# Local attention's probabilities turned on VectorE and by DMA in place of TensorE, on one Trainium2 core

## Chip, cores, metric

One core of one Trainium2 chip runs the whole program in one launch. The metric is device time in microseconds (us); a kernel's time is the median of its runs.

## What is computed

The reference is a two-layer encoder trunk (512 tokens of 1024 channels). Each layer normalises x, projects it with one input matrix, runs three branches on the pieces and adds the output projection back:

```python
h = rms_norm(x, g); z = h @ w_in
ya = neighbourhood_attention(aq, ak, av, rpb) * silu(ag)
yb = dilated_attention(rotary(bq), rotary(bk), bv) * silu(bg)
yc = conformer_conv(ca, cb, ...) * silu(cg)
x = x + concat([ya, yb, yc]) @ w_out
...
p = softmax(s.reshape(B, H, GRID_W, kh * kw), axis=-1)
return einsum('bhcij,ibhcjd->bhcd', p, v_win)
```

The neighbourhood ("local") attention has 4 heads: each token of the 8 x 64 grid looks at 8 rows and 16 columns around it, with a learned bias. The dilated attention has 6 heads over all 512 keys with a table of counts. A final RMSNorm ends the program. All of it is float32.

## The kernel before

**Tiles.** Every large product is made in three passes with the operands split in a high and a low part (`products`, L560 to L562: hi*hi, hi*lo, lo*hi), each pass a 128x128 weight block against 512 columns. A layer has 40 tiles: 29 of the input projection, 3 pointwise tiles of the convolution (29 to 31), 8 of the output projection (32 to 39). One tile is 24 matmuls of 512 columns (9 for a pointwise tile). In the last layer the output projection is turned round (`row_products`, L622 to L624: activations stationary, weights moving), in parts by pairs of weight blocks.

**Steps.** The queue of each engine is written out by hand. Nine tiles come first; from then on work goes by steps n = 0 to 42: TensorE does half a tile in each of the steps 0 to 39 (tile 9 + n // 2) and a pointwise tile in each of 40 to 42. Attention runs beside it, one unit a step: a unit is one head and 128 queries, 8 units are a pair of heads, 24 units of the dilated pairs 0 to 2 come first, then 16 of the local pairs 3 and 4 (units 24 to 39). For a local unit there are 256 keys.

**A unit's way.** TensorE makes the scores of four units at a time (`scores`, L670, after steps 3, 7, ... 35). VectorE adds bias or table and takes the maximum into a place of the ring `prob` (`maxima`, L1226, two units in every even step); ScalarE takes exp (`exps`, L846) and, one step later, scales by VectorE's reciprocal (`norm`, L853); two steps after its start TensorE turns the 128-column blocks of the probabilities into the bank `tp` (`turn`, L684), ScalarE copies them into `pT` (`empty_turn`, L871), and once a pair is there TensorE multiplies it with v (`values`, L703 for dilated pairs, L709 for local ones), after the steps 10, 18, 26 and 34 and, for the last pair, after step 42. VectorE multiplies the result by the gate (`gated`, L1247, L1251). The gated pair is split for the output projection by `y_hi` (ScalarE, L884) and `y_lo` (VectorE, L1266) in the order `K_ORDER`.

**Queues.** GpSimd's queue (POOL) loads the weights that aren't split on the chip: `load_hi` (L997) into `w_hi`, as soon as the tile five before is done; ScalarE negates a copy of it into `w_lo` (`negate`, L783); `load_lo` (L1002) then adds the weights onto it by DMA. The order in POOL's queue is fixed, each entry waits in its turn. SyncE's queue (SP) loads the raw weights of the first nine tiles into `pT`'s space, swaps rows for the rotary step (L464), stores v's turned blocks to DRAM and loads them back in another order (`store_v` L468, `load_v` L482), loads the biases of the local units into a ring of two (`load_bias`, L496) and in the last layer moves blocks of x (`move_x`, L489). `gf` (1024 columns) holds the final norm's gains, loaded ahead of the last layer's steps.

**VectorE's own turning** exists already for v (`vector.transpose`, L1148) and x (L1186): it turns blocks of 32x32 only; the blocks then have to change places by DMA.

The waits between engines are semaphores; VectorE's tile work is in `empty_tile` (L1103 to L1155), the convolution's taps in `conv_taps` (L1206).

Of the kernel before, what the change touches and what calls it, by code (L numbers as in the profile page):

```python
# [26 lines left out]
P = 128  # L27
SEQ = 512
# [50 lines left out]
DUNITS = DPAIRS * UPP  # L79
Y_OF_PAIR = [2, 3, 4, 0, 1]  # L80
K_ORDER = [2, 3, 4, 0, 5, 6, 1, 7]
# [7 lines left out]
NEG_TILE = 896  # L89
PREP = 8 + CT * TAPS + 4 * CT  # L90
# [13 lines left out]
X_ORDER = [list(range(KD))] + [K_ORDER] * (DEPTH - 1)  # L104
# [6 lines left out]
Y_BEFORE_W = 6  # L111
# [22 lines left out]
def build(nc, xT, w_in, w_pw, w_out, prm, gfin, nabias, lncnt, rope, out):  # L134
    with ExitStack() as ctx:
# [77 lines left out]
        bias_in = [sem(f"bias_in{i}") for i in range(2)]  # L213
# [34 lines left out]
        p_ready = sem("p_ready")  # L248
        t_ready = sem("t_ready")
# [132 lines left out]
        ROW_PARTS = [(0, [0]), (0, [1]), (0, [2]), (0, [3]), (1, [0]), (1, [1]), (1, [2, 3])]  # L382
        LAST = DEPTH - 1
# [10 lines left out]
        X_TILES = [(0, KD // 2), (KD // 2, KD)]  # L394
        X_BLOCKS = {26: 0}
# [42 lines left out]
        def _(sp):  # L438
# [44 lines left out]

            def move_x(half, i):
# [7 lines left out]
            def load_bias(l, un):  # L492
                b = un - DUNITS
# [16 lines left out]
            for l in range(DEPTH):  # L510
# [4 lines left out]
                if l == LAST:  # L515
                    sp.dma_start(gf[:, :], gfin).then_inc(gf_in, 16)
                for n in range(UNITS):
# [33 lines left out]
        def _(pe):  # L551
# [52 lines left out]
            def row_products(half, kps):  # L604
# [3 lines left out]
                elif kps[0] == 0:  # L608
                    pe.wait_ge(pt_ready, UNITS * DEPTH)
# [65 lines left out]
            def turn(l, n):  # L675
# [3 lines left out]
                if UNITS * l + n:  # L679

                    pe.wait_ge(pt_ready, UNITS * l + n)
                blocks = QT if g < DPAIRS else NKEY // P
                for k in range(blocks):
# [8 lines left out]
            def values(l, g):  # L692

                pe.wait_ge(pt_ready, UNITS * l + UPP * (g + 1))
# [10 lines left out]
                else:  # L705
                    for b in range(QT):
                        for half in range(2):
# [17 lines left out]
            for l in range(DEPTH):  # L725
# [15 lines left out]
                for n in range(SLOTS):  # L741
# [11 lines left out]
                    if n >= UPP + LAG and n % UPP == LAG and n < UNITS + LAG:  # L753
                        values(l, n // UPP - 1)
                    if LAG <= n < UNITS + LAG:
# [7 lines left out]
                values(l, PAIRS - 1)  # L763

                if l == LAST:
                    for half, kps in ROW_PARTS:
                        row_products(half, kps)
                    break
                c = N_IN + CT
                open_tile(l, c)  # L770
                products(c, act_hi, act_lo, order=K_ORDER, ready=(ylo_ready, KD * l))
                for c in range(N_IN + CT + 1, N_CH):
                    open_tile(l, c)
                    products(c, act_hi, act_lo, order=K_ORDER, used=act_used if c == N_CH - 1 else None)
# [3 lines left out]
        def _(act):  # L778
# [63 lines left out]
            def exps(l, n):  # L842
                w = SEQ if n < DUNITS else NKEY
# [694 lines left out]
```

## Time and profile before

| | before |
|---|---|
| time, median of 3 runs | 530.83 us (530.13 to 532.09) |
| the profiled execution's own time | 532.22 us |
| its span | 530.2 us |
| TensorE busy | 519.1 us (98%) |
| VectorE, ScalarE, GpSimd busy | 369.8, 279.3, 135.5 us |
| DMA moved | 92.32 MB, mean 174 GB/s |

The span is the stretch that the profiler saw; the 2.0 us between it and the execution's time lie outside. "Busy" is the time in which an engine works on at least one instruction. Engines overlap, so the shares don't add up; a share near the whole span says that shortening anything else is worth something only if this engine waits for it. A row of the profile's groups gives line, engine, operation, `out<-in` by the program's names, the count, busy time and mean duration, and behind the second bar how long the engine was idle just before such instructions and who ended that.

### The profile page before, as it was taken

The numbers are of one execution on the slowest core, as the hardware profiler recorded it, in microseconds if no ns is written. First come the engines' busy times: TensorE is split into PE (matmuls) and PEld (weight loads), VectorE is DVE, ScalarE is ACT, GpSimd is POOL, SyncE is SP. The second block draws the span as 40 slices with busy tenths as digits, with TensorE's granted clock in tenths as the row PEclk, the third lists the DMA queues.
The fourth block names the chain that finished last, engine by engine and source line by source line (L and its number), as shares of the span: only waits on it lengthen the run. The fifth ranks groups of instructions, "written<-read, shape, count | busy, mean of one in ns | idle before, by whom it ended". The sixth has DMA issues, their size and how long they took to land.

```text
span 530.2 us, 7797 instructions
## 1 busy us (share of the span) xinstructions
PE 519.1 (98%) x2846; PEld 406.2 (77%) x2846; DVE 369.8 (70%) x721; ACT 279.3 (53%) x535; POOL 135.5 (26%) x168
## 2 busy tenths in 40 slices
PE   8999999999999999999999999999999999999995
PEld 6888777587786887888888877877768678777884
DVE  6979697989984627611539969979999646546134
ACT  6713376565765558623423315756657656654314
POOL 0114232122133312324411233122122352123201
PEclk9999999999999999999999999999999999999999
DMA  8625688766675875799502479975785969669963
GB/s 285 270 79 138 158 196 203 164 168 160 151 194 137 216 176 117 182 279 269 155 6 99 108 168 217 205 174 133 169 185 137 229 163 253 133 133 231 229 139 159
DMA packets 39014, 92.32 MB, mean 174 GB/s; under 512 B 5440, under 2 KB 16960, under 8 KB 38976
## 3 DMA queue, kind: packets, MB, share of 16 engines
q0 software_dynamic: 17856, 61.09, 51.6%
q1 hardware_dynamic: 20832, 30.54, 17.8%
q8 instruction: 23, 0.38, 0.3%
q10 hardware_dynamic: 288, 0.19, 0.1%
q14 instruction: 15, 0.12, 0.1%
HBM read 81.84 MB, written 4.72 MB: 163 GB/s over the span
## 4 chain that ended last, share of the span: by engine, by line
PE 79%; DMA 9%; DVE 6%; issue 2%; SPq 1%; ACT 1%; POOL 1%; POOLq 0%; DVEq 0%; ACTq 0%
PE acc L560 17%; PE acc L562 17%; PE acc L561 17%; PE tp L684 5%; PE misc L703 4%; PE sc L670 4%; DMA sq<-sq 3%; DMA w_hi<-w_in 2%; DMA bias<-nabias 1%; PE sc L622 1%; PE sc L623 1%; PE sc L624 1%; DMA v_way<-vB 1%; PE sc L560 1%; PE sc L562 1%
## 5 line engine op out<-in xcount | busy, mean ns | idle before, releaser
L560 PE MATMUL acc<-act_hi,w_hi 128*128 128x512 f32 x480 | 195.2, 407 | 0.0
L562 PE MATMUL acc<-act_lo,w_hi 128*128 128x512 f32 x480 | 187.7, 391 | 0.0
L561 PE MATMUL acc<-act_hi,w_lo 128*128 128x512 f32 x480 | 187.3, 390 | 0.0
L562 PEld LDWEIGHTS acc<-act_lo,w_hi 128*128 128x128 f32 x480 | 90.1, 188 | 20.0
L560 PEld LDWEIGHTS acc<-act_hi,w_hi 128*128 128x128 f32 x480 | 90.2, 188 | 17.8 <-issue 1.4
L561 PEld LDWEIGHTS acc<-act_hi,w_lo 128*128 128x128 f32 x480 | 90.5, 188 | 17.0 <-issue 0.5
L783 ACT ACTIVATE w_lo<-w_hi 128x1024 fp32r<-128x1024 f32 (+1 forms) x62 | 61.9, 999 | 42.1 <-DMA w_hi<-w_out 37.3
L846 ACT ACTIVATE prob<-prob,nmx 128x512 f32<-128x512 f32 (+1 forms) x80 | 50.5, 631 | 38.6 <-DVE nmx L1226 38.6
L1206 DVE SCALAR_TENSOR_TENSOR y<-ub,par,y 128x512 f32<-128x512 f32 x90 | 67.3, 748 | 0.0
L1206 DVE SCALAR_TENSOR_TENSOR ub<-ub,par 128x512 f32<-128x512 f32 x84 | 65.8, 783 | 0.0
L1002 POOL DMA_DIRECT2D w_lo<-w_in x40 | 35.8, 895 | 113.1 <-ACT w_lo L783 112.4
L871 ACT ACTIVATE pT<-tp 128x512 f32<-128x512 f32 (+1 forms) x80 | 40.2, 502 | 44.5 <-PE tp L684 44.4
L853 ACT ACTIVATE prob<-prob,rden 128x512 f32<-128x512 f32 (+1 forms) x80 | 50.4, 630 | 22.9 <-DVE rden L1232 22.8
L684 PEld LDWEIGHTS tp<-ident,prob 128*128 128x128 f32 x256 | 30.6, 140 | 19.5 <-issue 9.8
L684 PE MATMUL tp<-ident,prob 128*128 128x128 f32 x256 | 42.4, 278 | 2.0 <-ACT pT L871 2.0
L1030 POOL TENSOR_TENSOR sq<-sq,cs 128x512 f32<-128x512 f32 x12 | 16.6, 1382 | 72.0 <-DMA sq<-sq 72.0
L1226 DVE CUSTOM_DVE_ANT_0 prob<-sc,cnt 128x512 f32<-128x512 f32 x48 | 31.4, 686 | 4.1 <-PE tp L684 3.1
L997 POOL DMA_DIRECT2D w_hi<-w_in x40 | 24.8, 621 | 31.3 <-PE acc L562 28.2
L1226 DVE CUSTOM_DVE_ANT_0 prob<-sc,bias 128x256 f32<-128x256 f32 x32 | 13.2, 421 | 27.8 <-DMA bias<-nabias 14.0
L1002 POOL DMA_DIRECT2D w_lo<-w_out x16 | 14.0, 873 | 45.6 <-ACT w_lo L783 45.6
L1285 DVE TENSOR_TENSOR w_lo<-pT,w_hi 128x1024 fp32r<-128x1024 f32 (+3 forms) x23 | 23.2, 1025 | 2.2 <-ACT w_hi L910 1.3
L1272 DVE TENSOR_TENSOR x<-x,acc 128x512 f32<-128x512 f32 x8 | 5.5, 687 | 26.1 <-PE acc L562 26.1
(143 smaller groups left out, 726.1 us busy)
## 6 DMA issues: line engine op xcount, KB each, us to landing
w_hi<-w_in POOLq DMA_DIRECT2D x40, 512.0 KB, 5.1
w_lo<-w_in POOLq DMA_DIRECT2D x40, 512.0 KB, 6.3
w_hi<-w_out POOLq DMA_DIRECT2D x16, 512.0 KB, 6.5
w_lo<-w_out POOLq DMA_DIRECT2D x16, 512.0 KB, 6.6
pT<-w_in SPq DMA_DIRECT2D x15, 512.0 KB, 5.3
bias<-nabias SPq DMA_DIRECT2D x32, 128.0 KB, 4.2
sq<-sq SPq DMA_DIRECT2D x48, 64.0 KB, 2.8
v_way<-vB SPq DMA_DIRECT2D x8, 256.0 KB, 3.1
```

The lines of the kernel that those rows point to most:

```text
L560: nc.tensor.matmul(to[:, :], w_hi[:, slot, k, :], a_hi[:, k, :], start=i == 0, stop=False)
L561: nc.tensor.matmul(to[:, :], w_lo[:, slot, k, :], a_hi[:, k, :], start=False, stop=False)
L562: last = nc.tensor.matmul(to[:, :], w_hi[:, slot, k, :], a_lo[:, k, :], start=False, stop=i == K - 1)
L684: last = nc.tensor.transpose(tp[:, k * P:(k + 1) * P], prob[:, n % PROBS, k * P:(k + 1) * P], ident[:, :])
L783: nc.scalar.activation(w_lo[:, c % SPL, 0:K, :], w_hi[:, c % SPL, 0:K, :].bitcast(F32), ACT.Copy, scale=-1.0).then_inc(neg_ready, 1)
L846: nc.scalar.activation(prob[:, n % PROBS, 0:w], prob[:, n % PROBS, 0:w], ACT.Exp, scale=-1.0, bias=nmx[:, n % 4:n % 4 + 1], accum_out=den[ ...
L853: nc.scalar.activation(prob[:, n % PROBS, 0:w], prob[:, n % PROBS, 0:w], ACT.Copy, scale=rden[:, n % 4:n % 4 + 1]).then_inc(p_ready, 1)
L871: nc.scalar.activation(pT[:, h, 0:kk, b * P:(b + 1) * P], tp[:, 0:kk * P].rearrange("p (k t) -> p k t", t=P), ACT.Copy).then_inc(pt_ready, 1)
L997: pool.dma_start(w_hi[:, c % SPL, 0:K, :], src).then_inc(whi_in[c % SPL], 16)
L1002: pool.dma_start(w_lo[:, c % SPL, 0:K, :], src, accum_op=ALU.add).then_inc(wlo_in[c % SPL], 16)
L1206: ins = nc.vector.scalar_tensor_tensor(out=dst, in0=src, scalar=w, in1=dst, op0=ALU.mult, op1=ALU.add)
L1226: nc.vector.tensor_tensor_reduce(out=prob[:, n % PROBS, 0:w], in0=sc[n % 4][:, 0:w], in1=add, scale=-1.0, scalar=3e38, op0=ALU.add, op1=AL ...
```

## The change

1. **Local units are turned without TensorE.** `turn` and `empty_turn` are left for the 24 dilated units. A local unit's probabilities (256 columns, now packed four to the first two places of `prob`, `p_of`) are turned in 32x32 blocks by VectorE (`turn_p`), two steps after the unit's start, into one of four places that hold a batch of four units (`p_turned`): the last two places of `prob` for batch 0, `sq` for 1, the last two places of `prob` again for 2, `zc` for 3. Batch 2 has to wait for batch 0's moves to land. From there 16 DMAs a batch, 32 partitions x 1 KB each (32 KB), put the blocks in their rows of `pT` (`p_there`, `move_p`): those of steps 30 to 45, 36 a layer by SP (`BY_SP`: 2, 2, 2 and 3 of every four) and 28 by POOL. 
2. **`values` of the local pairs move** and read `pT` in runs of 32 columns: pair 3 from after step 34 to after step 39, pair 4 from after step 42 into the output projection: in the first layer behind all but the last k of tile 32 and half of tile 33, whose remaining blocks come after it; in the last layer behind the second part of the rows. `K_ORDER` ends with pair 4's k, for these tiles and in the host's order of the last `w_out`. ScalarE negates two (first layer) or three (last) of the output's weight tiles ahead of pair 4's `y_hi` (`W_BEFORE_Y`).
3. **Biases in a ring of six**: the two old places and four in `gf`, from step 14 on. The final gains are therefore loaded into `gf` after half of the last output projection, ahead of that half's `move_x`.

```diff
-K_ORDER = [2, 3, 4, 0, 5, 6, 1, 7]
+K_ORDER = [2, 3, 4, 0, 5, 6, 7, 1]
+BIASES, BIAS_RING, BIAS_AT = UNITS - DUNITS, 6, 14
-Y_BEFORE_W = 6
+W_BEFORE_Y = [1, 2]
...
+        BY_SP = [QUADS // 2] * (LOCAL // BATCH - 1) + [QUADS - 1]
+        P_MOVES = {30 + 4 * q + i: (q, i) for q in range(LOCAL // BATCH) for i in range(QUADS)}
+        PV_LOCAL = 39
...
+        def p_of(n):
+
+            if n < DUNITS:
+                return prob[:, n % PROBS, :]
+            return prob[:, :, :].rearrange("p r t -> p (r t)")[:, NKEY * (n % BATCH):NKEY * (n % BATCH + 1)]
+
+        def p_turned(q):
+
+            return (prob[:, 2:4, :], sq, prob[:, 2:4, :], zc)[q][:, :, :].rearrange("p r t -> p (r t)")
+
+        def p_there(q):
+
+            return pT[:, :, :, :].rearrange("p r a t -> p (r a t)")[:, BATCH * NKEY * q:BATCH * NKEY * (q + 1)]
...
+            def move_p(l, q, i):
+                sp.wait_ge(p_blocks, LOCAL * l + BATCH * (q + 1))
+
+                sp.wait_ge(pv_done, PAIRS * l + DPAIRS)
+                for j in range(BY_SP[q]):
+                    sp.dma_start(p_there(q)[BLK * j:BLK * (j + 1), NKEY * i:NKEY * (i + 1)],
+                                 p_turned(q)[BLK * i:BLK * (i + 1), NKEY * j:NKEY * (j + 1)]).then_inc(p_moved[q], 16)
...
-                sp.wait_ge(m_ready, UNITS * l + (un - 1 if b >= 2 else DUNITS - 4))
-                sp.dma_start(bias[:, b % 2, :], nabias[l, b]).then_inc(bias_in[b % 2], 16)
+            def load_bias(l, b):
+                m = BIASES * l + b
+                if m >= BIAS_RING:
+
+                    used = m - BIAS_RING
+                    sp.wait_ge(m_ready, UNITS * (used // BIASES) + DUNITS + used % BIASES + 1)
+                sp.dma_start(bias_of(m), nabias[l, b]).then_inc(bias_in[m % BIAS_RING], 16)
...
-                pe.wait_ge(pt_ready, UNITS * l + UPP * (g + 1))
+                if g < DPAIRS:
+                    pe.wait_ge(pt_ready, DUNITS * l + UPP * (g + 1))
+                else:
+                    for q in range(UPP // BATCH * (g - DPAIRS), UPP // BATCH * (g - DPAIRS + 1)):
+                        pe.wait_ge(p_moved[q], P_MOVED[q] * (l + 1))
+                        pe.wait_ge(p_moved_too[q], P_MOVED_TOO[q] * (l + 1))
...
-                                                        pT[:, BLK * i // HD, half, b * P:(b + 1) * P],
+                                                        there[:, 2 * (b % 2) + BLK * i // HD, half],
...
-                    if LAG <= n < UNITS + LAG:
+                    if n == PV_LOCAL:
+                        values(l, DPAIRS)
+                    if LAG <= n < DUNITS + LAG:
                         turn(l, n - LAG)
...
+                for c, first, end in ((N_IN + CT, 0, KD - 1), (N_IN + CT + 1, 0, KD // 2), (N_IN + CT + 1, KD // 2, KD - 1)):
+                    if first:
+                        values(l, PAIRS - 1)
+                    else:
+                        open_tile(l, c)
+                    products(c, act_hi, act_lo, first, end, order=K_ORDER, ready=(ylo_ready, KD * l))
+                for c in range(N_IN + CT, N_IN + CT + 2):
+                    products(c, act_hi, act_lo, KD - 1, KD, order=K_ORDER, ready=(ylo_ready, KD * l))
...
+            def turn_p(l, n):
+                dve.wait_ge(p_ready, UNITS * l + n + 1)
+                q, u = divmod(n - DUNITS, BATCH)
+                if n == DUNITS:
+                    dve.wait_ge(t_ready, DUNITS * (l + 1))
+                if u == 0 and q == 2:
+                    dve.wait_ge(p_moved[0], P_MOVED[0] * (l + 1))
+                    dve.wait_ge(p_moved_too[0], P_MOVED_TOO[0] * (l + 1))
+                to = p_turned(q).rearrange("p (j u h t) -> p u h j t", j=QUADS, u=BATCH, t=BLK)[:, u]
+                nc.vector.transpose(to, p_of(n).rearrange("p (h j t) -> p h j t", j=QUADS, t=BLK)).then_inc(p_blocks, 1)
```

**How the queues move.** TensorE, first layer, from the last pass of step 35 into step 36 (tile 27's first matmul is the first of the closing rows). Before:

```order
L562 MATMUL acc<-act_lo,w_hi 128x512
L670 MATMUL sc<-k_hi,q_hi 128x256 x2
L670 MATMUL sc<-k_hi,q_lo 128x256 x2
L670 MATMUL sc<-k_lo,q_hi 128x256 x2
...
L684 MATMUL tp<-ident,prob 128x128 x2
L560 MATMUL acc<-act_hi,w_hi 128x512
```

and with the change (L607 to L609 are the three passes, L717 the scores):

```order
L609 MATMUL acc<-act_lo,w_hi 128x512
L717 MATMUL sc<-k_hi,q_hi 128x256 x2
L717 MATMUL sc<-k_hi,q_lo 128x256 x2
L717 MATMUL sc<-k_lo,q_hi 128x256 x2
...
L607 MATMUL acc<-act_hi,w_hi 128x512
```

The two-matmul turn between the scores and tile 27 is gone; so it is in each of the 16 steps of a layer that had one for a local unit.

VectorE, first layer, step 34 (from that step's maxima to the emptying of tile 25 by the last row, which frees the accumulator that tile 27 opens in). Before:

```order
L1226 ISA prob,nmx<-sc,bias 128x256
L1226 ISA nmx 128x1
L1226 ISA prob,nmx<-sc,bias 128x256
L1226 ISA nmx 128x1
L1232 RECIPROCAL rden<-den 128x1
L1365 TENSOR_TENSOR s_lo<-y,s_hi 128x512
L1237 SCALAR_TENSOR_TENSOR y<-th,y 128x512
L1103 SCALAR_TENSOR_TENSOR y<-acc,rstd 128x512
```

and with the change:

```order
L1300 ISA prob,nmx<-sc,gf 128x256
L1300 ISA nmx 128x1
L1300 ISA prob,nmx<-sc,gf 128x256
L1300 ISA nmx 128x1
L1317 RECIPROCAL rden<-den 128x1
L1313 STREAM_TRANSPOSE prob<-prob 128x2x4x32
L1455 TENSOR_TENSOR s_lo<-y,s_hi 128x512
L1322 SCALAR_TENSOR_TENSOR y<-th,y 128x512
L1175 SCALAR_TENSOR_TENSOR y<-acc,rstd 128x512
```

The added transpose is unit 32's, the first of batch 2: it holds the wait for all 16 moves of batch 0, and three instructions behind it stands the emptying of tile 25.

POOL, first layer, steps 30 to 33 (L1055 is `load_hi`, L1060 `load_lo`, L1094 POOL's share of `move_p`). Before:

```order
L997 DMA w_hi<-w_in 128x1024
L1002 DMA w_lo<-w_in 128x1024
L997 DMA w_hi<-w_pw 128x384
L1002 DMA w_lo<-w_in 128x1024
```

and with the change:

```order
L1055 DMA w_hi<-w_in 128x1024
L1094 DMA pT<-prob 32x256 x2
L1060 DMA w_lo<-w_in 128x1024
L1094 DMA pT<-prob 32x256 x2
L1055 DMA w_hi<-w_pw 128x384
L1094 DMA pT<-prob 32x256 x2
L1060 DMA w_lo<-w_in 128x1024
L1094 DMA pT<-prob 32x256 x2
```

Batch 0's last two moves on POOL stand behind the `w_lo` load of tile 28.

## Rows read from the trace of the kernel before

**Rows 1.** The page: busy time of TensorE, and its granted clock in 40 slices.
```profile
PE 519.1 (98%) x2846; PEld 406.2 (77%) x2846; DVE 369.8 (70%) x721; ACT 279.3 (53%) x535; POOL 135.5 (26%) x168
...
PEclk9999999999999999999999999999999999999999
```

**Rows 2.** Waits of TensorE over the whole span: waited for, us, times, longest.
```profile
PE tp L684 <- ACT pT L871: 2.0, 3, 1.0
...
PE misc L709 <- ACT pT L871: 0.8, 1, 0.8
```

**Rows 3.** Timeline of TensorE: start us, us, line, operation: one step with a turn, twelve matmuls without.
```profile
188.91 0.48 PE L560 MATMUL acc<-act_hi,w_hi 128*128 128x512 f32 x1
...
191.92 0.48 PE L560 MATMUL acc<-act_hi,w_hi 128*128 128x512 f32 x1
...
225.25 0.39 PE L560 MATMUL acc<-act_hi,w_hi 128*128 128x512 f32 x1
...
227.97 0.39 PE L560 MATMUL acc<-act_hi,w_hi 128*128 128x512 f32 x1
```

**Rows 4.** The same timeline: a pair's values with a turn behind, and without.
```profile
194.84 1.96 PE L709 MATMUL misc<-pT,v 128*32 128x128 f32 x64
...
197.24 0.39 PE L561 MATMUL acc<-act_hi,w_lo 128*128 128x512 f32 x1
...
220.51 1.95 PE L709 MATMUL misc<-pT,v 128*32 128x128 f32 x64
...
222.73 0.40 PE L561 MATMUL acc<-act_hi,w_lo 128*128 128x512 f32 x1
```

**Rows 5.** Timelines: VectorE's longest bias wait, TensorE's two waits in local stages, tile 27.
```profile
198.15 0.42 DVE L1226 CUSTOM_DVE_ANT_0 prob<-sc,bias 128x256 f32<-128x256 f32 x1 [5.53 <-DMA bias<-nabias]
...
201.54 0.41 PE L684 MATMUL tp<-ident,prob 128*128 128x128 f32 x2 [0.72 <-ACT pT L871]
201.71 0.48 PE L560 MATMUL acc<-act_hi,w_hi 128*128 128x512 f32 x1
...
478.11 1.95 PE L709 MATMUL misc<-pT,v 128*32 128x128 f32 x64 [0.80 <-ACT pT L871]
```

**Rows 6.** Windows of the first layer's local stage (us, busy PE, PEld, DVE, ACT, POOL, clock, DMA, GB/s).
```profile
165.00:214.00 49.00, 48.28 (x322) 37.60 (x315) 23.92 (x66) 29.14 (x75) 13.49 (x17) 1.00 0.66 154
```

**Rows 7.** The page's groups: VectorE's turning of v, its tile sums.
```profile
L1148 DVE STREAM_TRANSPOSE vB<-vT 128x512 f32<-128x512 f32 x8 | 5.7, 712 | 0.3
L1272 DVE TENSOR_TENSOR x<-x,acc 128x512 f32<-128x512 f32 x8 | 5.5, 687 | 26.1 <-PE acc L562 26.1
```

**Rows 8.** DMA issues by line, 400 to 440 us: duration ns on the queue, us to landing.
```profile
L489 SPq DMA_DIRECT2D x<-ub x16: 507/591/693, 424.8 to 438.6; - x16
...
DMA to landing us min/median/max: 1.9/5.1/6.5
```

**Rows 9.** Weight loads on POOL, tile 28's in layer one; its landing, and layer two's.
```profile
189.12 0.87 POOL L1002 DMA_DIRECT2D w_lo<-w_in  x1 [3.34 <-ACT w_lo L783]
...
DMA to landing us min/median/max: 8.0/8.0/8.0
...
L1002 POOL DMA_DIRECT2D w_lo<-w_in x1: 862/862/862, 448.0 to 448.0; - x1
...
DMA to landing us min/median/max: 5.7/5.7/5.7
```

**Rows 10.** Start of layer two's tile 27 on TensorE; median landings of the output projection's weights.
```profile
458.48 0.48 PE L560 MATMUL acc<-act_hi,w_hi 128*128 128x512 f32 x1
...
w_hi<-w_out POOLq DMA_DIRECT2D x16, 512.0 KB, 6.5
w_lo<-w_out POOLq DMA_DIRECT2D x16, 512.0 KB, 6.6
```

**Rows 11.** The end: SP's moves of x, and VectorE's first sum that waits for them.
```profile
502.08 12.61 SPq L489 DMA_DIRECT2D x<-ub  x16
...
516.20 0.69 DVE L1423 TENSOR_TENSOR pT<-acc,x 128x512 f32<-128x512 f32 x1 [9.14 <-DMA x<-ub]
```

More of the change, by code:

```diff
@@ L103 @@
 X_GROUPS = [(0, 1), (1, 2), (2, 3), (3, 5), (5, 6), (6, 8)]
[L104 removed]
+X_ORDER = [list(range(KD))] + [[2, 3, 4, 0, 5, 6, 1, 7]] * (DEPTH - 1)
 WARM = 10
@@ L212, in build @@
         par_in = sem("par_in")
-        bias_in = [sem(f"bias_in{i}") for i in range(2)]
+        bias_in = [sem(f"bias_in{i}") for i in range(BIAS_RING)]
         swap_in = sem("swap_in")
@@ L248, in build @@
         p_ready = sem("p_ready")
+        p_blocks = sem("p_blocks")
+        p_moved = [sem(f"p_moved{q}") for q in range(LOCAL // BATCH)]
+        p_moved_too = [sem(f"p_moved_too{q}") for q in range(LOCAL // BATCH)]
         t_ready = sem("t_ready")
@@ L531, in _ @@
                         move_x(*X_MOVES[n])
+                    if n in P_MOVES:
+                        move_p(l, *P_MOVES[n])
+                for n in range(UNITS, max(P_MOVES) + 1):
+                    move_p(l, *P_MOVES[n])
                 if l == LAST:
                     sp.wait_ge(tile_done, N_CH * LAST + OUT0 + KD // 2)
+                    sp.wait_ge(m_ready, UNITS * DEPTH)
+                    sp.dma_start(gf[:, :], gfin).then_inc(gf_in, 16)
                     for i in range(QUADS):
@@ L678, in turn @@
                 pe.wait_ge(p_ready, UNITS * l + n + 1)
[L679 to L683, printed above, removed]
+                if DUNITS * l + n:
+                    pe.wait_ge(pt_ready, DUNITS * l + n)
+                for k in range(QT):
                     last = nc.tensor.transpose(tp[:, k * P:(k + 1) * P],
@@ L974, in _ @@
                     y_hi(l, i)
-                    if i == Y_BEFORE_W - 1:
-                        split_next(l, N_IN + CT - 1)
+                    if i == KD - 2:
+                        for c in range(N_IN + CT - 1, N_IN + CT + W_BEFORE_Y[l]):
+                            split_next(l, c)
                 for c in range(N_IN + CT, N_CH):
-                    split_next(l, c)
+                    if c >= N_IN + CT + W_BEFORE_Y[l]:
+                        split_next(l, c)
                     if c > N_IN + CT and l < LAST:
@@ L1030, in rotate, with move_p @@
                 nc.gpsimd.tensor_tensor(zsw, zsw, cs[:, 1, :], ALU.mult).then_inc(t2_ready, 1)
+            def move_p(l, q, i):
+                pool.wait_ge(p_blocks, LOCAL * l + BATCH * (q + 1))
+                pool.wait_ge(pv_done, PAIRS * l + DPAIRS)
+                for j in range(BY_SP[q], QUADS):
+                    pool.dma_start(p_there(q)[BLK * j:BLK * (j + 1), NKEY * i:NKEY * (i + 1)],
+                                   p_turned(q)[BLK * i:BLK * (i + 1), NKEY * j:NKEY * (j + 1)]).then_inc(p_moved_too[q], 16)
             nc.gpsimd.memset(ident[:, :], 0.0).then_inc(consts, 1)
@@ L1068, in _ @@
                         root(l, MISC_LCOL)
+                    if n in P_MOVES:
+                        move_p(l, *P_MOVES[n])
                 for c in range(N_IN, N_CH):
                     hi_next(l, c)
+                    if c == N_IN + 2:
+                        for n in range(UNITS + 2, max(P_MOVES) + 1):
+                            move_p(l, *P_MOVES[n])
                     lo_next(l, c)
+                    if c == N_IN:
+                        move_p(l, *P_MOVES[UNITS + 1])
                     if c >= N_IN + CT + 2 and l < LAST:
```

72 lines of the change are left out of this document (37 added, 35 removed).

## Prediction

> **What bounds the kernel now.** I read the page first: TensorE is busy for 519.1 of 530.2 us and its granted clock is full (2.4 GHz) in every slice [rows 1], so time is TensorE's queue, and only two things can shorten it: fewer instructions there, or fewer waits. Then its waits: those for ScalarE's copies out of the turning bank sum to 2.8 us [rows 2]. The timelines place two of them in local stages, 0.72 us before tile 27 of the first layer and 0.80 us before the last pair's values in the second [rows 5]. The other three engines have room: in the first layer's local stage VectorE works 23.9 of 49 us, ScalarE 29.1, POOL 13.5 [rows 6]. Last, the DMA side, since the change puts work there.
>
> **The change part by part.** *Turning leaves TensorE.* A half tile is twelve matmuls. With a turn between, one half tile starts 191.92 - 188.91 = 3.01 us after the last; twelve matmuls without one take 227.97 - 225.25 = 2.72 us [rows 3]. A turn between two half tiles therefore costs 0.29 us, far less than its matmuls' printed durations, because they are pipelined. Next to a change of shape it costs less: from a pair's values to the second matmul behind them it is 197.24 - 194.84 = 2.40 us with a turn, 222.73 - 220.51 = 2.22 us without [rows 4], so 0.18 us. Of a layer's 16 local turns, five stand there (behind three score groups and two pairs' values, steps 26, 27, 31, 34, 35), eleven don't: 5 x 0.18 + 11 x 0.29 = 4.1 us a layer, **8.2 us** for both. All of it is on the path.
>
> *Waits that go.* The 0.72 us hangs on a bias: VectorE waited 5.53 us for one (ring of two), ScalarE's queue stood behind it, and TensorE's turn behind ScalarE's copy. Six places end that, and no turn is left to wait. The 0.80 us before the last values was a copy into `pT` behind ScalarE's negation; that copy is gone. Together **1.5 us**. Gain so far 9.7 us.
>
> *VectorE's turning.* 16 a layer of 256 columns. Turning 512 columns takes 0.71 us [rows 7]; half that is 0.36, with a fixed part I take 0.4 us, 6.4 us a layer (bounds 5.7 and 11.4, a full 0.71 each). It falls on an engine idle for 25 us of the stage [rows 6], so nothing by itself. ScalarE loses 16 copies a layer, worth nothing directly.
>
> *The moves.* 64 a layer of 32 KB, 2 MB beside the 154 GB/s x 49 us = 7.5 MB of the stage [rows 6]. The nearest row is x's moves, 64 KB: 0.59 us each on SP's queue and 1.9 to 6.5 us to landing, median 5.1 [rows 8]. Who waits? *Pair 3's values* have five steps more than before. *Pair 4's*: unit 39 is turned some 3 us after step 39's end; SP's twelve moves take 12 x 0.59 = 7 us and land by 3 + 7 + 2 to 5 = 12 to 15 us. TensorE arrives after pair 3's values (1.9), three pointwise tiles (3 x 2.0), seven k of tile 32 (4.8) and four of tile 33 (2.7), 15.5 us in; in the second layer the two row parts make it 18.8. I take zero, with little room in the first layer.
>
> *Batch 2's wait* is the place I look at hardest. VectorE may turn unit 32 in step 34 only when all moves of batch 0 have landed, and behind that stands the emptying of tile 25, whose accumulator tile 27 needs. TensorE wants tile 27 at 201.71 [rows 5], less ten turns (5 x 0.18 + 5 x 0.29 = 2.35), pair 3's values (1.9) and the 0.72: at 196.7. POOL's last two moves of batch 0 stand right behind tile 28's `w_lo`, issued at 189.1 and landed 8.0 us later [rows 9]; five turns earlier that is 187.9 and 195.9. If the moves land with it, VectorE turns (0.4) and goes through three more instructions of 0.7 by 198.4: TensorE stands for 1.7 us. If they land after x's median 5.1 us, it is 193.7 + 2.5 = 196.2 and costs nothing. I take 1.7, since both go through one queue. In the second layer tile 28's `w_lo` was issued at 448.0, took 5.7 us, and comes some 2 us earlier without VectorE's bias wait: 451.7 + 2.5 = 454.2, against tile 27 wanted at 458.48 - 2.35 - 1.9 = 454.2 [rows 9, 10]: zero. Bounds for both layers: 0 and 6 us. The trace shows a queue's order only in this form. The Trainium skill (DMA: Bandwidth & Descriptors, "Queues, rings and completion order") says each DMA engine takes turns between queues packet by packet and takes descriptors of one ring in order; by that POOL's moves do queue behind `w_lo` and SP's don't, which is the 1.7 us case; the landing of x's moves on SP in 5.1 us beside running weight loads agrees.
>
> *The output projection, first layer.* Tile 32 now follows the last pointwise tile at once. Its third k needs VectorE's pointwise and `y_lo`, 1.4 us and 0.4 of hand-overs after tile 31, and TensorE is there after 2 x 0.68: 0.4 us. Pair 4's gate, `y_hi`, `y_lo` take 0.7 each and 9 matmuls cover 2.0 of it: 0.2 us. Tile 32 then ends 0.68 us before tile 34 wants its bank, which VectorE frees in 0.69 [rows 7] and hand-overs: 0.3 us. Tile 37's weights may enter only after tile 32's late end: `w_hi` 6.5, negation 1.1, `w_lo` 6.6 [rows 10], POOL's issues about 2.5, in all 16.7 of the 17.0 us left; loads crowd there, so 0.4 us (bounds 0 and 3). Together 1.3 us. In the second layer the parts of rows are longer than these chains: zero.
>
> *The end.* `gf` (512 KB) now goes ahead of 16 moves of x, which took 12.6 us on SP and whose landing let VectorE's first sum go at 516.2 [rows 11]. A delay of up to 2 us there is regained, since TensorE brings a row block only every 2.72 us and VectorE needs some 1.6 for it: zero, bounds 0 and 1.
>
> **Sum.** 9.7 - 1.7 - 1.3 = 6.7 us. The profiled execution, 532.22 us, would be 525.5; it stood 1.4 us above the median of the runs, 530.83, and that comes to **524.1 us**.
>
> **The rivals.**
> *No wait worth naming* (batch 0 lands early in both layers, the projection's chains overlap): the full 9.7 us, 521.1. For it: POOL works only 13.5 of 49 us, and weights land long before use in the local stage. Against: the DMA waits of VectorE on biases show how late small transfers can come there [rows 5].
> *Moves late in both layers*: batch 0's last moves 3 us later than I count, in each layer, or tile 37's weights as much: 5 to 6 us more lost, about 529. For it: 28% more bytes into the stage, in 1 KB runs.
> *The strided operand*: the local values now read `pT` in runs of 32 columns that start 1 KB apart. If that doubled them, 4 x 1.96 = 7.8 us [rows 4], 532, no change. Nothing in the trace shows such an operand. The Trainium skill (SBUF: State Buffer, "Door 1: The DMA port swizzle") puts the penalty at leaving a 16-byte line, and these runs have 128 bytes; by that it is zero, and I give it little.
> *Slower*: the same place as batch 2's wait. Landings later than 194.2 in the first layer cost TensorE one for one, as VectorE's queue, with the maxima, reciprocals and tile sums in it, stands. If each POOL move waits out a weight load (8.0 us, one before and one behind, [rows 9]) and weights come late in turn, the stall is 1.7 + 8 us in the first layer and 6 in the second: 9.7 - 15.7 - 1.3 is 7.3 us slower, 538. It decides from 9.7 us of waits in all.
> *It doesn't do what it says*: waits for batches would have to keep TensorE as before; the order of the queues shows 32 turns gone, so no.
>
> **How the numbers follow.** About what a measurement can tell here is 0.5%, 2.7 us. My forecast (522.3 to 526) 0.44; no waits 0.20; moves late 0.18; strided operand 0.05; slower 0.07; the rest, pieces between these, 0.06. Faster by over 0.5% (below 528.2): 0.44 + 0.20, half of "late" and the rest's share: 0.77. Within: 0.15. Slower: 0.08. The range reaches from 520.3 (the full gain, and a little) to 528.8 (late in both layers).
>
> **What would show it.** Right: TensorE's turns down from 256 to 192 matmuls and half tiles of the local stage 2.72 us apart; a local pair's values still near 1.96 us; no wait of VectorE for biases; one wait of VectorE for a DMA into `pT` in step 34, and TensorE's wait for the emptied accumulator before tile 27 near 1.7 us in layer one; small waits around tiles 32 to 37. Wrong: no DMA wait at unit 32's turn (then 521), TensorE waiting for weights or before pair 4's values (late moves), VectorE turning at over 0.7 us each, or a last stretch, from the last matmul to the end, longer than before.

## The result, and the profile after it

| | before | with the change |
|---|---|---|
| time, median of 5 runs each, same chip | 531.1 us (530.13 to 532.09) | 539.66 us (537.56 to 540.22) |
| ratio | | 1.0139, 95% interval 1.0117 to 1.0162 |
| the profiled execution's own time; its span | 532.22; 530.2 us | 539.13; 537.2 us |
| TensorE busy | 519.1 us | 517.2 us |
| DMA moved | 92.32 MB | 96.51 MB |

Slower by 1.4%, where 524.1 us was predicted. The page of the changed kernel, against [rows 1]: 64 matmuls fewer, yet TensorE is busy for almost as long, and its granted clock is no longer full everywhere.

```profile
PE 517.2 (96%) x2782; PEld 402.8 (75%) x2782; DVE 379.1 (71%) x753; ACT 269.8 (50%) x503; POOL 164.7 (31%) x224
...
PEclk9999999999999998999999999999999999799999
```

Its waits of TensorE, against [rows 2] (waited for, us, times, longest). One new row holds 8.9 us, nearly all of the new waiting: it is for the accumulator that VectorE's L1175 (the emptying of a tile) frees.

```profile
PE acc L607 <- DVE y L1175: 8.9, 2, 5.8
PE misc L778 <- POOL ident L1102: 1.9, 1, 1.9
PE tp L730 <- ACT pT L928: 1.5, 2, 0.9
PE acc L607 <- DMA w_lo<-w_out: 0.4, 1, 0.4
PE sc L669 <- DMA w_lo<-w_out: 0.4, 1, 0.4
PE misc L763 <- issue: 0.3, 1, 0.3
```

Where it stands: VectorE's timeline from unit 32's turn in both layers (start us, us, then in brackets the idle time before and who ended it).

```profile
198.01 0.45 DVE L1313 STREAM_TRANSPOSE prob<-prob 128x256 f32<-128x256 f32 x1 [7.98 <-DMA pT<-prob]
198.38 0.65 DVE L1455 TENSOR_TENSOR s_lo<-y,s_hi 128x512 fp32r<-128x512 f32 x1
198.95 0.68 DVE L1322 SCALAR_TENSOR_TENSOR y<-th,y 128x512 f32<-128x512 f32 x1
199.55 0.68 DVE L1175 SCALAR_TENSOR_TENSOR y<-acc,rstd 128x512 f32<-128x512 f32 x1
...
460.93 0.45 DVE L1313 STREAM_TRANSPOSE prob<-prob 128x256 f32<-128x256 f32 x1 [9.59 <-DMA pT<-prob]
```

And TensorE's behind it: tile 27's first matmuls in both layers.

```profile
200.38 0.47 PE L607 MATMUL acc<-act_hi,w_hi 128*128 128x512 f32 x1 [3.06 <-DVE y L1175]
...
201.45 0.63 PE L607 MATMUL acc<-act_hi,w_hi 128*128 128x512 f32 x1
201.88 0.63 PE L608 MATMUL acc<-act_hi,w_lo 128*128 128x512 f32 x1
...
463.30 0.77 PE L607 MATMUL acc<-act_hi,w_hi 128*128 128x512 f32 x1 [5.84 <-DVE y L1175]
```

The place is the one predicted (unit 32's turn waits for batch 0's landings, the emptying of tile 25 stands three instructions behind it). TensorE also asks for tile 27 about when predicted: 32.99 us after the start of pair 2's values in both layers, where the prediction's 196.7 and 454.2 us are 32.8 after it. Two things are not as predicted: how long TensorE stands, 3.06 and 5.84 us, and what follows. Between 201.45 and 201.88 two matmuls lie 0.43 us apart, where 0.23 is usual. Windows of the change, two in each layer (us, busy time of PE, PEld, DVE, ACT, POOL, clock, DMA share, GB/s):

```profile
202.00:204.00 2.00, 2.00 (x6) 1.55 (x5) 2.00 (x7) 2.00 (x6) 0.00 (x0) 0.50 0.00 0
204.00:206.00 2.00, 2.00 (x10) 1.65 (x9) 1.72 (x5) 1.59 (x6) 1.57 (x3) 0.95 0.00 0
...
464.00:466.00 2.00, 2.00 (x7) 1.52 (x5) 2.00 (x8) 2.00 (x6) 0.00 (x0) 0.50 0.00 0
466.00:468.00 2.00, 2.00 (x8) 1.64 (x7) 1.83 (x5) 1.60 (x6) 0.65 (x2) 0.75 0.00 0
```

The granted clock is 0.50, 1.2 GHz, behind each idle stretch: TensorE is busy for all of the time there and does about half the work (6 and 7 matmuls of 512 columns in 2 us, against 10 and 11 in the same windows of experiment 5 below).

Why batch 0 was late: SP's queue in the first layer (start, us, line, the transfer).

```profile
180.43 0.34 SPq L502 DMA_DIRECT2D v_way<-vB  x1
180.86 1.16 SPq L523 DMA_DIRECT2D pT<-prob  x2
182.06 0.60 SPq L540 DMA_DIRECT2D bias<-nabias  x1
186.95 2.71 SPq L516 DMA_DIRECT2D v<-v_way  x4
189.76 1.75 SPq L523 DMA_DIRECT2D pT<-prob  x2
191.55 0.62 SPq L540 DMA_DIRECT2D bias<-nabias  x1
192.27 1.14 SPq L523 DMA_DIRECT2D pT<-prob  x2
```

`load_v` (L516) reads back what `store_v` (L502) wrote, and the store took 6.5 us to land, so SP stood until 186.95 with the second half of batch 0's moves behind it. The last pair was issued from 192.27 on and landed 5.1 us later, as VectorE's wait ended. POOL's last two had been issued from 188.92 on. In the second layer the store took 8.4 us; SP's last two moves went out at 455.47, POOL's at 449.07.

**The account**, by TensorE's own timeline in the profiled executions, cut where all kernels have the same instruction: pair 2's values, the first matmul of tile 29, the column of the second layer's norm. "Places" is the first experiment below, "no moves" the fourth.

| stretch, us | before | change | places | no moves |
|---|---|---|---|---|
| start to pair 2's values | 163.91 | 164.33 | 163.22 | 163.46 |
| to tile 29 (local stage, layer one) | 49.71 | 50.62 | 45.95 | 45.95 |
| to the next norm's column | 60.59 | 62.28 | 62.62 | 61.64 |
| to pair 2's values, layer two | 147.23 | 147.24 | 147.24 | 148.18 |
| to tile 29 (local stage, layer two) | 48.92 | 53.52 | 45.95 | 45.95 |
| to the end of the span | 59.84 | 59.21 | 58.52 | 58.62 |

The local stage without any wait is 45.95 us. The change's first one is 50.62 - 45.95 = 4.67 us longer: 3.06 idle and 1.6 of slow clock. Its second is 7.57 longer: 5.84 and 1.7. Together 8.9 us idle and 3.3 us of clock, 12.2 us. (The clock's part is what is left after the idle time; experiment 5 tests it.) The profiled execution of "places", 525.51 us, was the fastest of its six, 2.2 us below their median, so that column is a little too good.

### The profile page after: what moved, and what is told of

Same layout as the page of the kernel before. It is cut to its first block, busy times and chain, and to the rows that moved or that the text cites. A ratio compares the mean times of both kernels' runs of the same rounds, so it can differ in the third digit from the quotient of the medians.

```text
span 537.2 us, 7833 instructions
## 1 busy us (share of the span) xinstructions
PE 517.2 (96%) x2782; PEld 402.8 (75%) x2782; DVE 379.1 (71%) x753; ACT 269.8 (50%) x503; POOL 164.7 (31%) x224
## 2 busy tenths in 40 slices
DMA packets 44261, 96.51 MB, mean 180 GB/s; under 512 B 7488, under 2 KB 21312, under 8 KB 44224
## 4 chain that ended last, share of the span: by engine, by line
PE 72%; DMA 10%; DVE 9%; SPq 4%; issue 3%; POOL 1%; ACT 1%; POOLq 0%; DVEq 0%; ACTq 0%
PE acc L607 15%; PE acc L609 15%; PE acc L608 15%; PE misc L754 4%; PE tp L730 4%; PE sc L717 3%; DMA w_lo<-w_out 3%; DMA v_way<-vB 3%; DMA sq<-sq 3%; DMA pT<-prob 2%; PE sc L669 1%; DVE ub L1278 1%; PE sc L670 1%; PE sc L671 1%; PE sc L607 1%
## 5 line engine op out<-in xcount | busy, mean ns | idle before, releaser
L607 PE MATMUL acc<-act_hi,w_hi 128*128 128x512 f32 x480 | 195.8, 408 | 9.6 <-DVE y L1175 8.9
L609 PE MATMUL acc<-act_lo,w_hi 128*128 128x512 f32 x480 | 188.8, 393 | 0.0
L607 PEld LDWEIGHTS acc<-act_hi,w_hi 128*128 128x128 f32 x480 | 91.1, 190 | 32.3 <-issue 12.9
L609 PEld LDWEIGHTS acc<-act_lo,w_hi 128*128 128x128 f32 x480 | 90.9, 189 | 20.2
L608 PEld LDWEIGHTS acc<-act_hi,w_lo 128*128 128x128 f32 x480 | 91.2, 190 | 17.6 <-issue 0.5
L1060 POOL DMA_DIRECT2D w_lo<-w_in x40 | 36.0, 901 | 103.5 <-ACT w_lo L845 102.3
L1278 DVE SCALAR_TENSOR_TENSOR ub<-ub,par 128x512 f32<-128x512 f32 x84 | 64.6, 769 | 0.0
L928 ACT ACTIVATE pT<-tp 128x512 f32<-128x512 f32 x48 | 28.2, 587 | 26.1 <-PE tp L730 26.1
L1055 POOL DMA_DIRECT2D w_hi<-w_in x40 | 25.7, 644 | 32.4 <-PE acc L609 32.4
L730 PEld LDWEIGHTS tp<-ident,prob 128*128 128x128 f32 x192 | 22.4, 140 | 13.8 <-issue 7.3
L730 PE MATMUL tp<-ident,prob 128*128 128x128 f32 x192 | 29.7, 277 | 1.6 <-ACT pT L928 1.5
L902 ACT ACTIVATE th<-y 128x512 f32<-128x512 f32 x22 | 13.7, 622 | 28.2 <-DVE y L1175 28.2
L1060 POOL DMA_DIRECT2D w_lo<-w_out x16 | 14.3, 891 | 37.6 <-ACT w_lo L845 31.1
L754 PE MATMUL misc<-pT,v 128*32 128x512 f32 x192 | 21.8, 595 | 0.0
```

What stands on the lines that cost most here:

```text
L607: nc.tensor.matmul(to[:, :], w_hi[:, slot, k, :], a_hi[:, k, :], start=i == 0, stop=False)
L608: nc.tensor.matmul(to[:, :], w_lo[:, slot, k, :], a_hi[:, k, :], start=False, stop=False)
L609: last = nc.tensor.matmul(to[:, :], w_hi[:, slot, k, :], a_lo[:, k, :], start=False, stop=i == K - 1)
L730: last = nc.tensor.transpose(tp[:, k * P:(k + 1) * P], prob[:, n % PROBS, k * P:(k + 1) * P], ident[:, :])
L754: last = nc.tensor.matmul(ob[BLK * i:BLK * (i + 1), :], v_of(g, i, k), pT[:, BLK * i // HD, k, :], start=k == 0, stop=k == QT - 1)
L928: nc.scalar.activation(pT[:, h, :, b * P:(b + 1) * P], tp[:, :].rearrange("p (k t) -> p k t", t=P), ACT.Copy).then_inc(pt_ready, 1)
```

## The experiments

Ratios are to the kernel before, on the same chip; the change itself has 1.0139. One hundredth is 5.3 us.

**1. Batch 2's wait taken away, by exchanging the places of batches 2 and 3.**

```diff
-            return (prob[:, 2:4, :], sq, prob[:, 2:4, :], zc)[q][:, :, :].rearrange("p r t -> p (r t)")
+            return (prob[:, 2:4, :], sq, zc, prob[:, 2:4, :])[q][:, :, :].rearrange("p r t -> p (r t)")
...
-                if u == 0 and q == 2:
+                if u == 0 and q == 3:
```

> The change with the places of batches 2 and 3 exchanged: batch 2 is turned into zc, which is free, and batch 3 into the last two places of prob, so VectorE's wait for batch 0's landings moves from step 34 to step 38, some 12 us later, when they have long landed. Theory A (VectorE's stand before unit 32's turn is the main loss, twice: TensorE idle for 3.06 and 5.84 us before tile 27, and its clock at 1.2 GHz for a few us behind that, 1.5 and about 2.2 us more): both waits and both dips of the clock vanish, 12.6 us less, 527 us, ratio to the kernel before about 0.993. Theory B (the extra DMA traffic slows the landings of everything in the stage, and the wait only shows it first): the wait turns up before pair 3's or pair 4's values or before tiles 32 to 37 instead, and the time stays above 533 us. Theory C (the clock falls for another reason than the idle time, for instance the shorter mix of shapes): the granted clock still falls to 0.50 near 202 and 462 us, 535 us.

Measured: 527.74 us against 531.76, ratio 0.9922 (0.9904 to 0.9939), 2.2 hundredths below the change. Its waits of TensorE, all but the one at the start, and its windows of the two local stages:

```profile
PE misc L763 <- DMA pT<-prob: 1.3, 1, 1.3
PE tp L730 <- ACT pT L928: 0.9, 1, 0.9
PE acc L607 <- DVE x L1357: 0.2, 1, 0.2
```

```profile
165.00:214.00 49.00, 49.00 (x309) 38.53 (x302) 30.86 (x84) 28.85 (x67) 28.20 (x44) 1.00 0.81 185
428.00:480.00 52.00, 52.00 (x305) 42.31 (x304) 32.52 (x83) 29.49 (x63) 29.14 (x49) 1.00 1.00 241
```

Both idle stretches and both dips are gone, with all 128 moves still there and the DMA engines fuller than before (0.81 against 0.66 in [rows 6]). Theory A holds; B and C fall. What is left of B is 1.34 us before pair 4's values in the first layer. This version beats both kernels, the one before by 0.8%.

**2. Pair 4's v loaded later in SP's queue.**

```diff
-        V_LOADS = {5: 0, 13: 1, 17: 2, 24: 3, 32: 4}
+        V_LOADS = {5: 0, 13: 1, 17: 2, 24: 3, 38: 4}
```

> The change with one entry of SP's queue moved: pair 4's v is loaded back from DRAM at step 38 instead of 32, behind batch 0's moves instead of ahead of them. If SP's queue is what made batch 0 late (load_v held it until 186.95 us in the first layer and 451.67 in the second, waiting for store_v to land, and took 2.7 us itself), batch 0's moves on SP are issued 3 to 6 us earlier, VectorE's wait then ends with POOL's moves near 195.6 and 455.7, TensorE's two stands shrink from 3.1 and 5.8 us to about 0.7 and 1.0, the clock mostly stays up, and the time falls by 7 to 10 us, to 530 to 533. If POOL's moves behind tile 28's w_lo set the end, as the prediction had it, nothing changes: 539 to 540 us.

Measured: ratio 1.0005 (0.9986 to 1.0025), 531.78 us: 1.3 hundredths, 7 us, better than the change. Its timelines of VectorE and TensorE, and a window behind the longer stand:

```profile
195.73 0.45 DVE L1313 STREAM_TRANSPOSE prob<-prob 128x256 f32<-128x256 f32 x1 [5.57 <-DMA pT<-prob]
...
198.10 0.47 PE L607 MATMUL acc<-act_hi,w_hi 128*128 128x512 f32 x1 [0.64 <-DVE y L1175]
...
457.10 0.47 PE L607 MATMUL acc<-act_hi,w_hi 128*128 128x512 f32 x1 [2.75 <-DVE y L1175]
```

```profile
458.00:460.00 2.00, 2.00 (x11) 1.62 (x10) 2.00 (x9) 2.00 (x8) 0.00 (x0) 1.00 0.02 5
```

SP's last moves of batch 0 now go out at 185.17 and POOL's at 189.06, so POOL ends the wait. SP's queue was the later one in the change. The second layer's stand shrank only to 2.75 us, not 1.0; the clock stayed at 1.00 behind it.

**3. The bias ring alone**, on the kernel before.

```diff
+BIASES, BIAS_RING, BIAS_AT = UNITS - DUNITS, 6, 14
-        bias_in = [sem(f"bias_in{i}") for i in range(2)]
+        bias_in = [sem(f"bias_in{i}") for i in range(BIAS_RING)]
...
+                    sp.wait_ge(m_ready, UNITS * DEPTH)
+                    sp.dma_start(gf[:, :], gfin).then_inc(gf_in, 16)
```

> The kernel before with the third part of the change alone: biases in a ring of six, the final gains loaded later; turns stay on TensorE. The prediction's term for it: VectorE's wait of 5.53 us for a bias and TensorE's 0.72 us behind it go, 0.7 us in the first layer and up to 0.8 in the second: 529.4 to 530.4 us, ratio 0.997 to 0.9985. The rival: another producer ends TensorE's wait at once, or the later load of the gains delays the last rows, and the ratio is 0.9995 or more.

Measured: ratio 0.9979 (0.9964 to 0.9995), 1.1 us with an interval from 0.3 to 1.9. The prediction's 1.5 us for the waits lies in it, and both of TensorE's waits that it named, 0.72 and 0.80 us, are gone from the trace.

**4. The change without its moves.** Both `move_p` (only SP's is shown) issue nothing and every wait on them goes, VectorE's too. This kernel leaves out the data of the local pairs.

```diff
             def move_p(l, q, i):
+                return
...
-                        pe.wait_ge(p_moved[q], P_MOVED[q] * (l + 1))
-                        pe.wait_ge(p_moved_too[q], P_MOVED_TOO[q] * (l + 1))
+                        pe.wait_ge(p_blocks, LOCAL * l + BATCH * (q + 1))
```

> The change without its 128 moves: VectorE still turns the blocks, but they stay in their places and the local pairs' values read what lies in pT, so two of five pairs' values are left out of the result. No wait for moves is left on any engine. It prices what the turn's removal alone is worth. If the prediction's gain (8.2 us of turns, 1.5 of waits) and its 1.3 us of losses around the output projection were right and the rest of the loss is moves and their waits, it takes 530.8 - 8.4 = 522.4 us, ratio 0.984. If turns on TensorE were worth less than counted, or VectorE's turning costs something by itself, it takes 526 or more.

Measured: 525.67 us, ratio 0.9889 (0.9876 to 0.9903), 5.9 us gained where 8.4 were expected. It falls between the two lines of the expectation: turns were worth less than counted, and the next norm's stretch loses about what was counted. The table above gives both, worked out in the next section. The first experiment, with all moves, is 0.33 hundredths behind it: the moves and what is left of their waits cost about 1.8 us. The table doesn't show this, for the reason given below it.

**5. TensorE kept busy while it stands**, in the change itself, behind step 35's scores.

```diff
+                        if n == 35:
+                            pe.wait_ge(pt_ready, DUNITS * (l + 1))
+                            for _ in range(FILL[l]):
+                                nc.tensor.matmul(tp[:, :], act_hi[:, 0, 0:P], act_hi[:, 0, :], start=True, stop=True)
```

> The change as it is, with matmuls put into TensorE's queue where it stands idle before tile 27: 12 of 512 columns in the first layer (12 x 0.227 = 2.7 us of the 3.06 it stood) and 23 in the second (5.2 of 5.84), into a bank that nothing reads. They wait for nothing, so they only fill the idle time. Theory A (the clock fell because TensorE was idle): the granted clock stays 1.00 behind both places, the 1.5 and 2.0 to 2.5 us of matmuls at 1.2 GHz go, and the kernel is 3 to 4 us faster than the change, 535.5 to 536.7 us, although VectorE's waits stay as they are. Theory B (the dips belong to the stage, not to the idle time): the clock dips as before and the time stays within 0.5 us of the change's, or grows.

Measured: ratio 1.0101 (1.0076 to 1.0126), 536.68 us, 2.0 us better than the change; the two intervals overlap, so the time alone doesn't decide, and the windows behind both places do:

```profile
202.00:204.00 2.00, 2.00 (x10) 1.68 (x9) 1.91 (x5) 1.60 (x5) 0.57 (x1) 1.00 0.00 0
...
464.00:466.00 2.00, 2.00 (x11) 1.65 (x10) 2.00 (x9) 2.00 (x7) 0.00 (x0) 1.00 0.06 16
```

The clock stays full, with VectorE's waits hardly changed (16.3 us in two; 17.6 in the change). The two local stages take 48.70 and 51.18 us against the change's 50.62 and 53.52, 4.3 us less. Of these 3.3 are the clock; the added matmuls take 2.75 and 5.23 us and no wait is left behind them, where TensorE stood for 3.06 and 5.84, which is the rest. In the profiled execution 3.0 of the 4.3 are lost again around pair 4's values in the first layer, 2.37 us idle and then the values themselves at half clock:

```profile
229.13 3.57 PE L764 MATMUL misc<-pT,v 128*32 128x128 f32 x64 [2.37 <-issue]
```

A window within these values:

```profile
230.00:232.00 2.00, 2.00 (x45) 2.00 (x40) 0.00 (x0) 0.00 (x0) 0.00 (x0) 0.50 0.71 141
```

So A holds for the clock, and the smaller gain has its place. That wait is longer than the change's 0.28 us for two reasons in the traces: TensorE asked 16.3 us after the start of pair 3's values instead of 17.0, and SP's last three moves, issued at the same distance from it in both, took up to 6.1 us to land instead of 4.7. Why they landed later stays open.

**6. Batch 3's moves shared evenly between the queues**, on the first experiment.

```diff
-        BY_SP = [QUADS // 2] * (LOCAL // BATCH - 1) + [QUADS - 1]
+        BY_SP = [QUADS // 2] * (LOCAL // BATCH)
```

> The change with exchanged places (as in the first experiment) and batch 3's moves shared 8 and 8 between SP and POOL instead of 12 and 4. TensorE stood 1.34 us there before pair 4's values in the first layer. If SP's queue sets that (12 moves of 0.68 us behind unit 39's turn at 210.3 us, the last issued at 218.5), SP is through 2.7 us earlier and the wait goes: 1.3 us less than the first experiment, 526.4 us. The rival: POOL's extra four moves, 0.6 us each, put the output projection's weights back by 2.4 us, and TensorE waits at tiles 35 to 37 for them instead: no gain, or up to 1 us slower.

Measured: ratio 0.995 (0.9932 to 0.9967), 0.3 hundredths, 1.5 us, worse than the first experiment, with intervals that just overlap. The median is worse than the rival's "up to 1 us", and the waits are the rival's, but the one before pair 4's values did not go either. POOL's eight moves, and TensorE's waits:

```profile
215.16 4.31 POOL L1094 DMA_DIRECT2D pT<-prob  x8
```

```profile
PE misc L763 <- issue: 2.1, 1, 2.1
...
PE sc L669 <- DMA w_lo<-w_out: 1.6, 1, 1.6
...
PE acc L607 <- DMA w_lo<-w_out: 1.0, 2, 0.7
```

The moves stand right behind a 512 KB load of `w_hi` and take 8.5 us to land (10.7 for the load). So pair 4's values wait for 2.06 us instead of 1.34, and the weights behind the moves come late in turn.

**7. The first experiment with two biases instead of six.**

```diff
-BIASES, BIAS_RING, BIAS_AT = UNITS - DUNITS, 6, 14
+BIASES, BIAS_RING, BIAS_AT = UNITS - DUNITS, 2, 14
```

> The change with exchanged places, but biases in a ring of two again: its third part undone. TensorE has no local turn left that could wait behind a late bias, so the question is whether the ring is still worth anything. If bias loads, now queued on SP between the moves, come late, VectorE stands for them up to 5 us as before, and batches, scores and tile 27 behind it: 1 to 4 us slower than the first experiment, 529 to 532. If VectorE's slack (idle for about half of the stage) takes it up: the same, within 0.5 us.

Measured: 567.53 us, ratio 1.0674 (1.0638 to 1.071). Both lines of the expectation missed it by far. Its waits of VectorE and one of TensorE's:

```profile
DVE prob L1300 <- DMA bias<-nabias: 58.7, 13, 8.3
```

```profile
476.03 0.77 PE L607 MATMUL acc<-act_hi,w_hi 128*128 128x512 f32 x1 [7.69 <-DVE y L1175]
```

With moves and v's loads in SP's queue, a bias that can be asked for only two units ahead comes late 13 times in 32 units, by 4.5 us in the mean (in the kernel before 8 times, 14.0 us in all). TensorE's idle time, without the wait at the start, grows from 2.4 to 33 us, and its mean granted clock falls from 0.996 to 0.973. The ring, worth 1.1 us alone, is worth 40 us beside the moves: the parts of this change don't add.

**8 and 9. POOL's order: batch 0's last two moves ahead of tile 28's `w_lo`.** Run 8 has it on top of experiment 2, run 9 on the change itself.

```diff
                     if n < UNITS and n % 2 == 0:
                         hi_next(l, tile_at(n)[0])
+                    if n == 33:
+                        move_p(l, *P_MOVES[n])
                     if n < UNITS and n % 2 == 1:
                         lo_next(l, tile_at(n)[0])
...
-                    if n in P_MOVES:
+                    if n in P_MOVES and n != 33:
                         move_p(l, *P_MOVES[n])
```

> The second experiment (pair 4's v loaded at step 38) and one exchange in POOL's queue: batch 0's last two moves stand ahead of tile 28's w_lo instead of behind it. In the second experiment the wait of unit 32's turn ended when those two landed, 6 to 7 us after they were issued, and TensorE still stood 0.64 and 2.75 us. If they are late because the 512 KB of w_lo go ahead of them in the same queue (the prediction's mechanism), they are issued 1.5 to 3 us earlier, land by 193 and 452 us, TensorE's two waits vanish, and the time is 3 us below the second experiment: 528 to 529 us, ratio 0.994. If they are late whatever the order, because the DMA engines are full (busy share 0.9 to 1.1 there), or because the moves on SP land no earlier, the stands shrink by no more than 1 us in sum, and the ratio stays at 0.998 to 1.001.

> The same exchange in POOL's queue in the change itself, v's load left where it was. If SP's queue alone set the end of the wait in the change (its last moves of batch 0 went out at 193.4 and 456.6 us, 4 us behind POOL's last), nothing changes: ratio 1.0139 as the change, within 0.2%. If POOL's share did, as the prediction had it, 3 to 6 us are gained.

Measured: run 8 has 527.23 us, ratio 0.992 (0.9892 to 0.9948); run 9 has 1.015 (1.0124 to 1.0176). With the change and experiment 2 that makes a square:

| | v's load at step 32 | at step 38 |
|---|---|---|
| POOL's moves behind `w_lo` | 1.0139 | 1.0005 |
| ahead of it | 1.015 | 0.992 |

POOL's order alone is worth nothing, since SP's moves are later still; once SP's are early, it is worth 0.85 hundredths, 4.5 us. In run 8 TensorE's wait before tile 27 is down to this, in the second layer:

```profile
453.04 0.47 PE L607 MATMUL acc<-act_hi,w_hi 128*128 128x512 f32 x1 [0.21 <-DVE y L1177]
```

How POOL's place acts is to be read from its queue in experiment 2:

```profile
185.37 0.99 POOL L1094 DMA_DIRECT2D pT<-prob  x2
188.46 0.93 POOL L1060 DMA_DIRECT2D w_lo<-w_in  x1 [2.09 <-ACT w_lo L845]
189.06 1.35 POOL L1094 DMA_DIRECT2D pT<-prob  x2
```

`w_lo` waits for ScalarE's negation, and the moves behind it wait too. In run 8 all four go out from 184.51 on. Counted from pair 2's values in each run, the last pair of them is issued 2.7 us earlier in the first layer and 3.2 in the second, and VectorE's wait ends 2.9 and 2.5 us earlier. The median landing went only from 5.6 to 5.1 us in the first layer and from 6.5 to 5.8 in the second. It was the wait ahead of the moves in the queue that cost, more than the bytes ahead of them.

## Why the prediction was wrong

The step that failed is *batch 2's wait*, "I take 1.7" in the first layer and "zero" in the second. The prediction found the mechanism, its place and the engines in the right order. It then asked when POOL's last two moves would land, and never asked the same of SP's, though half of batch 0 is SP's. SP's rows of v's way were there to be read in the trace of the kernel before; its first layer has `load_v` 7.1 us behind the store that it waits for:

```profile
181.25 0.33 SPq L468 DMA_DIRECT2D v_way<-vB  x1
...
188.35 1.75 SPq L482 DMA_DIRECT2D v<-v_way  x4
```

Put in order, the moves of steps 32 and 33 stand behind `load_v` of step 32. In the change the store takes 6.5 and 8.4 us to land, and with SP's moves that late the stands are 3.06 us (1.7 taken) and 5.84 (zero taken). POOL's part alone, by experiment 2, would have been 0.64 and 2.75 us, so the zero for the second layer was wrong for POOL too. The Trainium skill says (DMA: Bandwidth & Descriptors, "Anatomy of one DMA") that a DMA's semaphore wait is spent on the issuing sequencer, before dispatch; both queues here agree, SP standing until 186.95 in the change for the store's landing and POOL until 188.46 in experiment 2 for ScalarE. The prediction cited another section of that page, on the order within a ring, and put SP outside the danger by it; by experiments 2, 8 and 9 the time of issue decided, and going ahead of `w_lo` instead of behind it shortened landings by 0.5 to 0.7 us.

The second failure is a term that the sum did not have: what an idle TensorE costs afterwards, 1.6 and 1.7 us at 1.2 GHz. Experiment 5, with TensorE kept busy, has no such dip there. The prediction read the clock as full everywhere and never asked what a new stand would do to it. The Trainium skill (TensorE: Matmul & The Clock Gate, "HAM oscillation") warns of just this, idle gaps that bring the clock down for the next burst; the two dips agree.

The other terms:

*Turns, 8.2 us.* The stretches give 49.71 - 0.72 - 45.95 = 3.04 us in the first layer and 48.92 - 45.95 = 2.97 in the second, for 14 turns each: 0.215 us a turn, 6.9 for 32. The right mechanism, 1.3 us too large. The step that failed is 3.01 - 2.72 = 0.29 [rows 3]: 3.01 was one interval. Three others of the kernel before, by the last matmul of a half tile, make (213.25 - 204.33) / 3 = 2.97, and from the last matmul ahead of a turn to the second behind it, against two usual distances, a turn costs 0.23. With that and the 0.18 beside a change of shape the 14 turns make 2.97 us, near the 3.04 and 2.97 measured.

```profile
204.33 0.39 PE L562 MATMUL acc<-act_lo,w_hi 128*128 128x512 f32 x1
...
213.25 0.39 PE L562 MATMUL acc<-act_lo,w_hi 128*128 128x512 f32 x1
```

*Waits that go, 1.5 us.* Right within experiment 3's interval.

*VectorE's turning, 0.4 us each.* 0.42 to 0.45, and it costs TensorE nothing: experiments 1 and 4 have no wait of TensorE in the local stages. The strided operand costs nothing: a local pair's values take 1.95 us, as in [rows 4].

*Pair 4's values, zero, "with little room in the first layer".* 0.28 us in the change, 1.34 in the first experiment: there the values could start 224.90 - 207.28 = 17.6 us after pair 3's, and TensorE asked for them after 16.3. The moves took 2 us and more over the 12 to 15 counted.

*The output projection, 1.3 us.* Without moves the first layer's stretch grows by 61.64 - 60.59 = 1.05 us, and two turns of 0.215 are gone from it: 1.5 us. The sum was right, its parts partly not: the bank of tile 34 0.17 us (0.3 taken), nothing at tile 32's third k (0.4), but 0.44 for tile 32's own `w_lo`. These waits make 0.61 of the 1.5; another 0.7 are breaks of 0.2 to 0.3 us without a named wait, at the first matmuls of tiles 32 and 34 and where tile 32's last k follows, which the prediction didn't count. That the sum came out is in part luck. In the change it is 1.69 + 0.43 = 2.1 us. In the second layer zero was taken. The last stretch should have shrunk by 0.8 + 0.43; it did by 59.84 - 59.21 = 0.63, so 0.6 us were lost, 0.37 of them for a late `w_lo`. In the first experiment it shrank by 1.32, so neither the order of the rows nor the later `gf` costs anything.

Put together for the profiled executions: 6.9 + 0.72 + 0.8 gained, 12.2 + 2.1 + 0.6 lost, and 0.4 us before pair 2's values, where nothing changed. That is 6.9 us slower, as 539.13 - 532.22 is.

*The rivals.* The slower one, 538 us at 0.07, named this place and came near the time. It set the bound at 9.7 us of waits, and there were 8.9 and 3.3 of clock; it thought of POOL's weight loads, where SP's own queue did it. Without the two stands the change takes 525.51 us in the first experiment's profiled execution, near the 525.5 of the sum. That is luck: turns 1.3 us too large, 1.2 us more lost around the projection, with the wait before pair 4's values, and against them no 1.7 us for a stand and a start 0.7 us shorter. The median of its runs is 527.74.

## What to carry to other kernels

When a wait for transfers is added to an engine, write down for every queue that carries one of them what stands ahead of its last issue and what those entries wait for; the latest queue counts, and mending another one gains nothing. Look for a buffer that needs no wait before tuning the queues: exchanging two places gave here what two queue changes gave together. Ask of a stand of TensorE whether matmuls at low clock follow it; here they cost 1.6 and 1.7 us more. When part of a change seems worth a microsecond alone, try it once with the rest in place.

## What was unexpected of the hardware

The clock's fall did not follow from the length of the idle time alone. TensorE fell to 0.50 after idle times of 3.06 and 5.84 us in the change and 2.37 us in experiment 5, and stayed at 1.00 after 2.75 us in experiment 2 and 2.1 us in experiment 6. Keeping TensorE busy with matmuls that nobody needs held it at 1.00 through VectorE's wait. The DMA engines' busy share of 1.00 over the 52 us of the second local stage, in the first experiment, left TensorE without a wait there.
